# A two-block language-model layer stack: the order of the first loads, and the first norm's squares added behind all splits

## The reference, cut to what matters

```python
def rms_norm(x, g):
    x32 = x.astype(jnp.float32)
    y = x32 * lax.rsqrt(jnp.mean(x32 * x32, axis=-1, keepdims=True) + EPS)
    return (y * g.astype(jnp.float32)).astype(x.dtype)
...
        h = rms_norm(x, norm_mix[l])
        proj = jnp.einsum('bsd,dc->bsc', h, w_in[l])
```

## Time and profile before

| | us |
|---|---|
| median of 3 runs | 2860.39 (2859.12 to 2863.31) |
| time of the profiled execution | 2862.94 |
| its span in the trace | 2861.1 |
| TensorE busy | 2661.2 (93%) |
| VectorE, ScalarE, GpSimd busy | 1364.2, 896.9, 1135.6 |

### The profile page before, as it was taken

One profiled execution on the slowest core, in us unless ns is written; L12 is line 12 of the kernel. 1 busy time (PEld: TensorE's weight loads), 2 busy tenths in 40 slices (PEclk: granted clock), 3 DMA queues, 4 the chain that ended last, 5 costly groups with the idle time before them and its releaser, 6 DMA issues.

```text
span 2861.1 us, 30409 instructions
## 1 busy us (share of the span) xinstructions
PE 2661.2 (93%) x11658; PEld 2047.2 (72%) x11658; DVE 1364.2 (48%) x2108; ACT 896.9 (31%) x1366; POOL 1135.6 (40%) x887
## 2 busy tenths in 40 slices
PE   7999999999999999899899999999956678999998
PEld 6877767888788887667666778888822255788886
DVE  4226686434433214947656433321589875433311
ACT  3443354222222222244455222222333134322221
POOL 4222335544444443432222444444434440444442
PEclk9999999999999999999999999999978788999999
DMA  3212122332222222211111223223200020233232
GB/s 132 66 45 69 55 83 74 96 96 92 96 89 96 90 94 96 65 53 52 45 45 52 90 91 96 96 89 96 77 0 1 5 78 1 89 96 96 88 94 77
DMA packets 62288, 210.30 MB, mean 74 GB/s; under 512 B 6848, under 2 KB 10048, under 8 KB 62016
## 3 DMA queue, kind: packets, MB, share of 16 engines
q1 hardware_dynamic: 61136, 205.02, 22.5%
q10 hardware_dynamic: 1008, 3.34, 0.4%
HBM read 206.24 MB, written 2.10 MB: 73 GB/s over the span
## 4 chain that ended last, share of the span: by engine, by line
PE 77%; DVE 16%; ACT 3%; issue 3%; POOL 1%; DMA 0%; DVEq 0%; ACTq 0%; SPq 0%; POOLq 0%
PE ps L582 22%; PE ps L583 21%; PE ps L584 21%; DVE T L1829 1%; PE ps L603 1%; PE ps L604 1%; PE ps L605 1%; DVE A L2146 1%; PE ps L1062 1%; PE ps L1071 1%; PE ps L893 1%; DVE A L2156 1%; DVE A L2155 1%; DVE A L1720 1%; PE ps L921 1%
## 5 line engine op out<-in xcount | busy, mean ns | idle before, releaser
L532 POOL TENSOR_TENSOR w_lo<-w_raw,w_hi 128x512 fp32r<-128x512 f32 (+4 forms) x818 | 1040.0, 1296 | 1588.6 <-ACT w_hi L1109 1588.5
L582 PE MATMUL ps<-H,w_hi 128*128 128x512 f32 x1896 | 769.3, 406 | 37.1 <-POOL w_lo L532 33.2
L583 PE MATMUL ps<-H,w_hi 128*128 128x512 f32 x1896 | 755.4, 398 | 0.0
L584 PE MATMUL ps<-H,w_lo 128*128 128x512 f32 x1896 | 755.0, 398 | 0.0
L1109 ACT CAST w_hi<-w_raw 128x1024 fp32r<-128x1024 f32 (+4 forms) x409 | 403.1, 991 | 617.8 <-DMA w_raw<-in_weights_dram 604.5
L582 PEld LDWEIGHTS ps<-H,w_hi 128*128 128x128 f32 x1896 | 359.8, 190 | 135.8 <-issue 35.5
L582 PE MATMUL ps<-split,w_hi 128*128 128x512 f32 x1032 | 414.3, 401 | 14.9 <-POOL w_lo L532 6.0
L584 PEld LDWEIGHTS ps<-H,w_lo 128*128 128x128 f32 x1896 | 359.4, 190 | 86.9
L583 PEld LDWEIGHTS ps<-H,w_hi 128*128 128x128 f32 x1896 | 360.2, 190 | 82.2 <-issue 1.7
L583 PE MATMUL ps<-split,w_hi 128*128 128x512 f32 x1032 | 410.7, 398 | 0.0
L584 PE MATMUL ps<-split,w_lo 128*128 128x512 f32 x1032 | 410.6, 398 | 0.0
(11 more groups left out here) (344 smaller groups left out, 2777.2 us busy)
## 6 DMA issues: line engine op xcount, KB each, us to landing
w_raw<-in_weights_dram SPq DMA_DIRECT2D x331, 512.0 KB, 3.5
w_raw<-in_weights_dram SPq DMA_DIRECT2D x48, 448.0 KB, 3.2
X<-in_xt_dram SPq DMA_DIRECT2D x4, 512.0 KB, 9.3
w_raw<-in_weights_dram SPq DMA_DIRECT2D x16, 128.0 KB, 2.0
out_dram<-A SPq DMA_DIRECT2D x8, 256.0 KB, 2.1
w_raw<-in_weights_dram SPq DMA_DIRECT2D x8, 192.0 KB, 2.3
w_raw<-in_weights_dram SPq DMA_DIRECT2D x6, 256.0 KB, 2.6
A<-in_w_gates_dram ACTq DMA_DIRECT2D x1, 1024.0 KB, 5.9
```

The costliest lines, as they stand in the source:

```text
L532: sub = nc.gpsimd.tensor_tensor(w_lo[:, p % NS, c], w_raw[:, p % NS, c], w_hi[:, p % NS, c].bitcast(F32), ALU.subtract)
L582: mm_(ps[:, bank, :], r(wh), xh, start=(k == 0), stop=False)
L583: mm_(ps[:, bank, :], r(wh), xl, start=False, stop=False)
L584: mm = mm_(ps[:, bank, :], r(wl), xh, start=False, stop=(k == kt - 1))
```

## The change

Three orders are changed, and nothing is added or left out. SyncE requests panel 0 ahead of X's first quarter. ScalarE requests the constants and the masks after the casts of panels 0 and 1 instead of ahead of them. VectorE makes all eight splits first, and then the seven additions of the squares.

```diff
@@ SyncE
+            panel(0)
             x_part(0)
-            panel(0)
             panel(1)
             x_part(1)
             x_part(2)
@@ ScalarE
             act.dma_start(V_[:], vectors).then_inc(s_vec, 16)
+            hi_to(2)
             act.dma_start(C_[:], consts).then_inc(s_con, 16)
             act.dma_start(MASKS32, masks).then_inc(s_msk, 16)
-            hi_to(2)
             for k in range(KT):
                 act.wait_ge(s_xin[k // 2], 16)
                 square("mix", k, X[:, k, :])
@@ VectorE
             for k in range(KT):
                 dve.wait_ge(s_xin[k // 2], 16)
                 scaled(HX, k, X[:, k, :], vec("norm_mix", k), s_h)
-                if k:
-                    add_square("mix", k)
+            for k in range(1, KT):
+                add_square("mix", k)
```

## The result

The changed kernel takes 2867.89 us (median of 8 runs, 2862.13 to 2871.53), the kernel before 2861.0 beside it (8 runs). The ratio is 1.0025, with a 95% interval of 1.0014 to 1.0036: slower by 7.1 us, between 4.0 and 10.3. The profiled execution took 2866.39 with a span of 2864.6.

What follows compares the result with a forecast made beforehand. TensorE, busy nearly all the time, was taken as the bound, so the start of its gapless stretch at tile 2 (30.25 us) counts. Terms +4.1 - 0.3 + 2.1 give +5.9 on the median 2860.4: 2866.3 us, range 2862.3 to 2869.

Steps and rivals of the forecast that it cites:

- the band of 2865 to 2867.5: Whole kernel: the main forecast's range of times in us, around 2866.3, given chance 0.57.
- More of the same: Rival at the start: VectorE blocked in full, or restart at 2.6 and X's quarters late; 2867.5 to 2869 us, chance 0.16.
- Requests: First loads: panel 0 lands at 5.1 us, X's first quarter at 6.4, panel 1 at 7.7.
- Collision: First two tiles' splits: GpSimd's four instructions come first and lengthen VectorE's splits by 3.4 us, bounds nothing and 5.1.
- Turns: Behind the splits: square and addition alternate every 1.50 us; last square at 29.7 against 25.62, +4.1 us.
- From the last square to tile 2: Panel 2's preparation: 4.63 us before, shortened by 0.3 as the last addition no longer runs beside GpSimd; tile 2 near 34.1.
- Clock: Tile 2's first matmuls: slow restart after TensorE idles about 9 us, +2.1 us, bounds 0 and 2.6.
- the bound of 2.6: Upper limit for the slow restart at tile 2, from eight fp32 matmuls: 6.31 us after a pause, 3.67 at high rate.
- Behind it is only a shift: After tile 2's start: nothing later waits for an absolute time and could take the shift back.
- the additions' order without the earlier data would be worse still: Start of the kernel: moving only the additions, without the earlier data, would lose more than the +4.1 us at the last square.

Runs made afterwards that it cites:

- e5: Changed kernel with a second buffer for the first norm's squares, so a square waits for the addition before the last; ratio to the kernel before 1.0007.
- e3: Changed kernel with panels 2 and 3 cast behind the second square instead of the eighth; ratio to the kernel before 1.0000, first logits at 106.46 us.
- e2: Kernel before with only the additions moved behind all splits, loads in the old order; ratio to the kernel before 1.0014, first logits at 110.48 us.
- e12: Kernel before with seven square buffers and additions behind the splits, loads in old order; first logits at 101.68 us, ratio 0.9983 when timed again.
- e11: Kernel before with seven square buffers and nothing else changed; one execution, first logits at 106.34 us, 1.5 us later than before.
- e8: Changed kernel with a buffer of its own for each of seven squares; ratio to the kernel before 0.9991, again 0.9985; first logits at 100.62 us.
- e1: Changed kernel with the additions back between the splits, new load orders kept; ratio to the kernel before 0.9999, first logits at 104.04 us.
- e4: Changed kernel with 36 extra matmuls into an unused bank between tiles 1 and 2; ratio to the kernel before 1.0008, first logits at 108.31 us.
- e10: Changed kernel with X's first quarter again requested ahead of panel 0; one execution, first logits at 109.02 us.
- e7: New load orders, additions between splits as before, panels 2 and 3 cast behind the second square; one execution, first logits at 106.38 us.

## Why the prediction was right

The forecast was 2866.3, +5.9; measured are 2867.89, +7.1 by the ratio, +6.35 at the logits. The chain of waits is the one that was forecast. The median lies 0.4 us above the band of 2865 to 2867.5 that had most of the chance, in *More of the same*, and of that rival's causes the slow restart came true. By its steps:

- **Requests.** Panel 0's cast 5.02 (forecast 5.1), X's first split 6.53 (6.5), panel 1's cast 7.74 (7.8, with panel 1 landing at 7.7). They were worked out from the landing times and the rate before, and these carried over to the new order.
- **Collision.** 3.2 us for 3.4, and GpSimd's four instructions 5.76 us. The Trainium skill's rule (SBUF - State Buffer, "Who interferes with whom"), taken as a charge of four whole instructions, would have given 5.1; measured are 3.2. That GpSimd, once first, keeps VectorE out is as the rule says, by the 1.16 to 1.64 us of the four splits.
- **Turns.** First addition 21.15 (21.4), turns of 1.50 (1.50), last square 29.52 (29.7). e5 shows that it is the wait for the one buffer: with two the turn is 0.84 and tile 2 comes 4.3 us earlier. e3 shows that panel 2 was held only by its place behind the squares.
- **From the last square to tile 2.** 4.28 us, as forecast (4.63 - 0.3 = 4.33). Tile 2 at 33.80 for 34.1: +3.55 where the sum had +3.8.
- **Clock.** The term that was mis-sized: +2.1 forecast, 2.8 measured (77.40 us from tile 2 to the logits, against 74.60 before). It lies just over the bound of 2.6 that I had from the fp32 matmuls. 14 spacings were slow; the forecast had some 10, under the 12 slow matmuls of the kernel's start.

Part of the closeness is luck. The sum had 0.25 us too much at tile 2 and 0.7 too little for the clock, and these partly cancel. "Behind it is only a shift" holds for 75 us and not for the program: the change is 6.4 us late up to 179 us, 7.9 from 184 us on, 8.4 at 1905 us, 5.0 at 2440 us and 3.5 at the end of the span, mostly by two stretches (last section) that no term of the sum had.

One sentence of the prediction was wrong: that the additions' order without the earlier data would be worse still. e2 is 0.7 us better than the change at the logits. Its tile 2 is 0.6 later, as the sentence has it, but its restart costs 1.5 us and not 2.8.

The gain that the new order aims at is real: tiles 0 and 1 end 4 us earlier. It was turned into a wait because ScalarE, which makes the squares, also prepares the next panel and copies the tiles. In the kernel before, the turns of square and addition were hidden between the splits; behind them they were not. Free ScalarE of that wait and the same order is worth 4.7 us: e12 against e11, 101.68 for 106.34. The loads' order is worth about 1 us at the logits in either company (e8 against e12 1.1, e1 against before 0.8).

## What to carry to other kernels

Before work is moved behind other work on one engine, ask which engine takes turns with it through a single buffer, and what stands behind that engine's half in its own program. Here deferred additions held up a weight cast that stood behind the squares in ScalarE's program; a buffer for each square, in space that was free at that time, turned a loss of 6 us at the first logits into a gain of 3 to 4. And a pause in front of TensorE is to be priced with its slow restart: it made 2.8 of 6.35 us.

## What was not expected of the hardware

**The restart's cost doesn't grow with the pause.** The time from tile 2's first matmul to the logits is 74.6 us without slow matmuls (before, e1, e4). With a pause of 4.16 us in front it was 77.0 (e5), with 6.17 us 76.0 (e10), with 8.21 us 76.1 (e2), with 9.18 us 77.4 (the change): 1.4 to 2.8 us, in no order. The shortest of these pauses, e3's 2.64 us, cost the most, 3.1 us. The pause of 1.58 us cost nothing (before, e1). The slow spacings were 12 in e5, 7 in e10, 7 in e2 and 14 in the change, each one execution of a kernel of its own, so what decides their number stays open. The Trainium skill, TensorE: Matmul & The Clock Gate, section "What's actually happening", says that the number of slow matmuls at a kernel's start differs from run to run of one kernel. The traces agree: at the start of e8's kernel 13 and 11 matmuls took 0.63 us or more in its two executions, at the start of e12's 12 and 10.

**A pause of 1.27 us costs 1.5 us in half of the executions.** TensorE stands still for 1.27 us at the same instruction in all 14 traces, in the kernel before at 180.05, in the changed one at 186.41:

```profile
180.05 0.36 PE L603 MATMUL ps<-w_hi,H 128*128 128x256 f32 x1 [1.27 <-issue]
```

```profile
186.41 0.36 PE L603 MATMUL ps<-w_hi,H 128*128 128x256 f32 x1 [1.27 <-issue]
```

The windows of the same matmuls behind it, before and after:

```profile
180.00:183.80 3.80, 3.75 (x32) 3.78 (x33) 0.00 (x0) 0.90 (x1) 2.52 (x2) 1.00 0.21 84
```

```profile
186.40:191.66 5.26, 5.25 (x32) 5.26 (x33) 0.00 (x0) 0.85 (x1) 2.52 (x2) 0.68 0.14 55
```

The granted clock stays at 1.00 in the one and is 0.68 on average in the other, and the same work takes 1.5 us longer. Seven traces have this (the change, e4, e5, e7, both of e8's kernel and e11), seven don't (before, e1, e2, e3, e10 and both of e12's). It takes more from e8 than its lead of 1.1 us over e12. What decides it is open.

**One later stage carries much of the scatter.** Between the first addition to X in down2 and the first one in out3, a stretch in which TensorE is often idle, the same instructions take longer or shorter. The windows of the kernel before and of e12, each between those two additions:

```profile
1905.00:2437.00 532.00, 424.83 (x1496) 279.35 (x1495) 330.73 (x508) 155.27 (x277) 206.20 (x173) 0.88 0.13 39
```

```profile
1904.00:2429.00 525.00, 415.49 (x1496) 272.79 (x1495) 331.02 (x509) 155.32 (x277) 206.30 (x173) 0.90 0.13 39
```

The two are 7 us apart: TensorE is busy 9 us longer at a granted clock of 0.88 than at 0.90, while the busy times of VectorE, ScalarE and GpSimd agree. In the changed kernel's profile the stretch took 528 us, in e5's 525, in the kernel before 532, in the other experiments' 532 to 533. This is the larger part of why a shift of 6.4 us at 105 us, by then 8.4, comes out as 3.5 in the spans of two executions (2861.1 and 2864.6), and why the experiments are read at the logits. Whether a kernel's start decides which of the values it gets, or chance, is open: e12's two profiles have 525 and 528, e8's two 532 and 532.
